# Order of the RWKV-7 projections and of the work between them and the recurrence

## The chip, the cores and the metric
The kernel runs on one core of a Trainium2 chip. The time is device microseconds of one launch. The time before is the median of three runs.

## The reference
One step of a 4-layer recurrent decoder trunk in float32, for a prompt of 256 tokens and 8 samples of 4 tokens that share the weights (288 token columns in the kernel, D = 1024). The layers' token mixers are RWKV-7, gated DeltaNet, HGRN2 and RWKV-7 again; each is followed by a gated convolution FFN. Only the two RWKV-7 mixers (layers 0 and 3, j = 0 and 1 in the code) matter here:

```python
mixed = x[None] + (prev - x)[None] * P['rwkv_mix'][j][:, None, None, :]
xr, xw, xk, xv, xa, xg = (mixed[s] for s in range(6))
r, k, v = jnp.einsum('sbtd,sde->sbte', jnp.stack([xr, xk, xv]), P['rwkv_w_rkv'][j])
w_log = -softplus(-(w0 + tanh(xw @ w1) @ w2)) - 0.5
a = sigmoid(a0 + (xa @ a1) @ a2)
v = v + (v_first - v) * sigmoid(v0 + (xv @ v1) @ v2)        # layer 3 only
g = sigmoid(xg @ g1) @ g2
kk = _l2norm(hd(k * k_k))
k = k * (1 + (a - 1) * k_a)
decay = jnp.exp(-jnp.exp(w_log))
o, S = _rwkv7_scan(hd(r), hd(decay), hd(k), hd(v), kk, hd(a), S0)
bonus = jnp.sum(hd(r) * hd(k) * r_k, -1, keepdims=True) * hd(v)
```

## The kernel before, in words
Activations lie in SBUF as eight row tiles of 128 features by 288 columns; a whole activation is 128 x 2304. A 1024 x 1024 weight is read as four slabs of 128 x 2048 (256 output columns, 1 MB). `weight_plan` fixes the order of all slabs; SyncE loads them in that order into a ring of four slots, each as soon as TensorE is through with the slab four places earlier. A large projection is made with three rounded matmuls: ScalarE copies a slab's high half (`split_hi`, tile `w_hi`, two slots), VectorE subtracts it to get the low half (`split_lo`, tile `w_lo`), and TensorE makes high x high, high x low and low x high for each of the 8 x 2 blocks (`three`, lines 532 to 534). ScalarE evacuates each output tile (`evac`). The input of such a projection, a mixture of the normed input and its shifted neighbour, is split by VectorE in the same way (`split_tiles`). The small projections (w1/w2 for the decay, a1/a2, g1/g2, in layer 3 also v1/v2 for the gate of v) are plain float32 matmuls (`linear_slab`, line 483), the second of each pair waiting for ScalarE's activation of the first.

Every engine's order is the order of its code, in `rwkv(j)` of each engine's block. Before, it is: v, (v1, v2 in layer 3), k, r as twelve slabs, then w1, w2, a1, a2, g1, g2; then the chain that makes the operands of the recurrence. VectorE scales k by `k_k` (`kk_raw`); ScalarE squares it; TensorE sums per head with a block matrix of ones (`tile_stats`, line 554), ScalarE takes logarithm and exponential (`head_rstd`, signal `rk_ready`); VectorE makes the running sums of the decay's logarithm (`tensor_tensor_scan`), the corrected key K, the normed key and B; three exponentials of the running sums come from ScalarE (`e_excl`, `e_incl`, `e_neg`), with VectorE's products and the eight tiles of the bonus between them. `operands_ready` releases TensorE's first products of the recurrence (`invert64`, line 725). The RWKV layers' sample states are loaded by GpSimd's queue, pair by pair, as the recurrence uses them up. GpSimd builds masks at the start of the program and keeps the shift rows; it has no arithmetic in an RWKV layer.

## Time and profile before

| | us |
|---|---|
| median of 3 runs (2378.93 to 2386.48) | 2384.39 |
| profiled execution, own time | 2372.57 |
| its span | 2370.8 |
| TensorE busy (matmul) | 2054.4 (87%) |
| VectorE busy | 1490.4 (63%) |
| ScalarE busy | 959.7 (40%) |
| GpSimd busy | 537.0 (23%) |

The span runs from the first to the last instruction. Busy times are shares of the whole program; a stage is read in windows of the timeline. The granted clock is TensorE's, as a share of its full speed; its mean here is 0.927. Layer 0's RWKV mixer begins the program; layer 3's begins at about 1700 us. An arrow names what ended an idle time.

### The profile page before, as it was taken

The page shows a single profiled execution, that of the slowest core. Times are in us where ns is not written, and L with a number is a line of the kernel's source. Part 1 is how long each engine was busy: PE and PEld are TensorE (multiplying, and loading weights), DVE is VectorE, ACT ScalarE, POOL GpSimd, SP SyncE. Part 2 cuts the span into 40 slices and gives each one's busy share as a digit, 9 for nine tenths or more (in the row PEclk, how much of TensorE's full clock was granted, in tenths as well). Part 3 has the DMA queues.
Part 4 walks back from the last instruction along what each step waited for, and adds up shares of the span by engine and source line. Part 5 has one row for each costly group of instructions (what it writes and reads, how often), then busy time and mean ns, then how long its engine had stood idle before and what let it go on. Part 6 is the DMA issues. An engine that isn't in the chain of part 4 may idle for free.

```text
span 2370.8 us, 54800 instructions
## 1 busy us (share of the span) xinstructions
PE 2054.4 (87%) x23495; PEld 1899.2 (80%) x23495; DVE 1490.4 (63%) x2234; ACT 959.7 (40%) x1640; POOL 537.0 (23%) x931
## 2 busy tenths in 40 slices
PE   4885996899989788799989697999888599869997
PEld 4865885899959677699989676999778388759997
DVE  4547535799368556589645765897465654458972
ACT  3341124555346502455445325555433411344543
POOL 8000000255014121046200550363000000004530
PEclk8987998999989889899999899999989789989999
DMA  4520112354424332244535253454433101224552
GB/s 123 158 63 4 29 37 87 110 171 161 149 81 131 98 99 80 81 160 161 165 115 156 88 168 97 129 171 153 142 112 100 36 21 31 66 72 143 161 165 76
DMA packets 272064, 257.77 MB, mean 109 GB/s; under 512 B 30692, under 2 KB 267206, under 8 KB 271822
## 3 DMA queue, kind: packets, MB, share of 16 engines
q1 hardware_dynamic: 221520, 219.63, 28.9%
q10 hardware_dynamic: 45774, 20.31, 3.2%
q0 software_dynamic: 4528, 14.33, 2.2%
q8 instruction: 186, 3.05, 0.5%
q14 instruction: 56, 0.46, 0.1%
HBM read 235.69 MB, written 18.54 MB: 107 GB/s over the span
## 4 chain that ended last, share of the span: by engine, by line
PE 52%; DVE 7%; ACT 3%; issue 2%; ACTq 0%; POOL 0%; DMA 0%; DVEq 0%; POOLq 0%
PE wide L532 6%; PE bank L532 6%; PE wide L534 6%; PE wide L533 6%; PE bank L534 6%; PE bank L533 6%; DVE arena L2448 3%; PE wide L543 2%; PE wide L752 1%; PE wide L767 1%; DVE arena L2445 1%; ACT arena L1709 1%; PE wide L764 1%; ACT w_hi L1709 1%; PE wide L554 1%
## 5 line engine op out<-in xcount | busy, mean ns | idle before, releaser
L2448 DVE TENSOR_TENSOR w_lo<-ring,w_hi 128x2048 fp32r<-128x2048 f32 (+1 forms) x208 | 471.1, 2268 | 323.1 <-ACT w_hi L1709 320.5
L532 PE MATMUL wide<-arena_rounded,w_hi 128*128 128x288 f32 x1632 | 496.5, 304 | 74.3 <-DVE arena_rounded L2448 57.6
L532 PE MATMUL bank<-arena_rounded,w_hi 128*128 128x288 f32 x1632 | 496.3, 304 | 33.2 <-issue 20.8
L533 PE MATMUL bank<-arena_rounded,w_hi 128*128 128x288 f32 x1632 | 491.3, 301 | 0.0
L534 PE MATMUL bank<-arena_rounded,w_lo 128*128 128x288 f32 x1632 | 490.2, 300 | 0.0
L533 PE MATMUL wide<-arena_rounded,w_hi 128*128 128x288 f32 x1632 | 489.9, 300 | 0.0
L534 PE MATMUL wide<-arena_rounded,w_lo 128*128 128x288 f32 x1632 | 488.3, 299 | 0.0
L1709 ACT ACTIVATE w_hi<-ring 128x2048 fp32r<-128x2048 f32 (+1 forms) x208 | 391.3, 1883 | 138.8 <-PE bank L534 71.4
L532 PEld LDWEIGHTS wide<-arena_rounded,w_hi 128*128 128x128 f32 x1632 | 314.1, 192 | 85.5 <-issue 81.0
L532 PEld LDWEIGHTS bank<-arena_rounded,w_hi 128*128 128x128 f32 x1632 | 316.0, 194 | 36.1 <-issue 35.4
L2445 DVE SCALAR_TENSOR_TENSOR arena<-arena,pv 128x304 f32<-128x304 f32 (+3 forms) x528 | 311.2, 599 | 37.1 <-PE wide L534 21.4
L533 PEld LDWEIGHTS bank<-arena_rounded,w_hi 128*128 128x128 f32 x1632 | 316.0, 194 | 0.5
L534 PEld LDWEIGHTS bank<-arena_rounded,w_lo 128*128 128x128 f32 x1632 | 316.3, 194 | 0.0
L534 PEld LDWEIGHTS wide<-arena_rounded,w_lo 128*128 128x128 f32 x1632 | 315.0, 193 | 0.0
L533 PEld LDWEIGHTS wide<-arena_rounded,w_hi 128*128 128x128 f32 x1632 | 314.5, 193 | 0.4
L1709 ACT ACTIVATE arena<-wide 128x256 f32<-128x256 f32 (+3 forms) x348 | 109.9, 346 | 430.2 <-PE wide L534 258.2
L2448 DVE TENSOR_TENSOR arena<-arena 128x32 f32<-128x32 f32 (+7 forms) x311 | 189.4, 635 | 62.3 <-ACT arena L1709 48.5
L1709 ACT ACTIVATE arena<-bank 128x32 f32<-128x32 f32 (+3 forms) x291 | 83.9, 323 | 322.5 <-PE bank L534 192.6
L1709 ACT ACTIVATE arena<-arena 128x288 f32<-128x288 f32 (+5 forms) x341 | 173.8, 542 | 57.8 <-DVE arena L2448 36.0
L3478 POOL COPY arena<-arena 128x16 f32<-128x16 f32 (+1 forms) x200 | 155.6, 778 | 183.4 <-DVE arena L2445 169.8
L3519 POOL DMA_DIRECT2D sraw<-in_state_rwkv_wkv x32 | 22.1, 694 | 528.1 <-PE wide L1042 281.9
L3487 POOL COPY arena<-arena 128x2 f32<-128x2 f32 (+1 forms) x200 | 92.1, 461 | 178.1 <-ACT arena L1709 172.0
(464 smaller groups left out, 2687.3 us busy)
## 6 DMA issues: line engine op xcount, KB each, us to landing
ring<-in_ffn_w_up SPq DMA_DIRECT2D x88, 1024.0 KB, 5.1
ring<-in_ffn_w_down SPq DMA_DIRECT2D x32, 896.0 KB, 4.8
ring<-in_rwkv_w_rkv SPq DMA_DIRECT2D x24, 1024.0 KB, 5.2
ring<-in_ffn_w_down SPq DMA_DIRECT2D x16, 1024.0 KB, 5.4
ring<-in_gdn_w_in SPq DMA_DIRECT2D x16, 1024.0 KB, 5.7
ring<-in_hgrn_w_in SPq DMA_DIRECT2D x16, 1024.0 KB, 5.5
ring<-in_rwkv_w_o SPq DMA_DIRECT2D x8, 1024.0 KB, 5.8
sraw<-in_state_rwkv_wkv POOLq DMA_DIRECT2D x32, 128.0 KB, 3.0
```

Source lines behind the costliest of these rows:

```text
L532: nc.tensor.matmul(out, wh, xh, start=first, stop=False)
L533: nc.tensor.matmul(out, wh, xl, start=False, stop=False)
L534: return nc.tensor.matmul(out, wl, xh, start=False, stop=last)
L543: mm = nc.tensor.matmul(bk[b][:, 0:T], ones[:, :], src[:, c, :], start=(c == 0), stop=(c == KC - 1))
L554: mm = nc.tensor.matmul(bk[b][:, 0:T], weights[:, :], src[:, c, :], start=True, stop=True)
L752: mm = nc.tensor.matmul(bk[b][rows, c * 64:c * 64 + 64], LT[g][rows, c, :], TF[g][rows, c, :], start=True, stop=True)
L764: nc.tensor.matmul(bk[b][rows, c * 32:c * 32 + 32].rearrange("p (b t) -> p b t", t=h), tt_[g][rows, c, :], halves(EL[g][rows, c, :], h, 0) ...
L1709: return nc.scalar.activation(out, in_, f, bias=bias, scale=scale)
L2445: return V.scalar_tensor_tensor(out=out, in0=a, scalar=s, in1=b, op0=o0, op1=o1)
L2448: return V.tensor_tensor(out, a, b, op)
L3478: G.tensor_copy(s[:, :, 0:lead], hv[:, :, :, c]).then_inc(signal("hist_in"), 1)
L3487: G.tensor_copy(lv[:, 0, :, c], ext[:, NPR:NPR + lead])
```

## The change
The plan and the code of each engine put w1/a1, w2/a2 and g1 first, then k, (v1,) v and r, and g2 last. The weights of v2 are no longer part of a slab: ScalarE's queue loads them into the free tiles `rs` and `nu`. The head statistics of k stand in TensorE's order behind the first v slab. The squares take `k_k` as ScalarE's scale, without VectorE's scaled copy, and ScalarE makes 1 + (a - 1) k_a. VectorE makes the mixtures for k and r in three small tiles (`mixture`) and their splits straight from there; its products, scans and the normed key stand between the low halves of the slabs. The constant 0.6065 goes into the exponentials' scale. The products of K and B with the negative exponential, and in layer 3 the three operations that mix v with the first layer's v, are made by GpSimd on 128 x 2304 tiles. The operands A and R lie in `AR` by operand, tile and column, no longer interleaved by chunk, and R's product with the inclusive exponential is made tile by tile, each followed by its bonus product.

```diff
     def rwkv(j):
-        plan.extend(("rkv", j, 2, m) for m in range(4))
-        if j:
-            plan.append(("v12",))
-        plan.extend(("rkv", j, 1, m) for m in range(4))
-        plan.extend(("rkv", j, 0, m) for m in range(4))
         plan.append(("wa1", j))
         plan.append(("wa2", j))
         plan.append(("g1", j))
+        plan.extend(("rkv", j, 1, m) for m in range(4))
+        if j:
+            plan.append(("v1",))
+        plan.extend(("rkv", j, 2, m) for m in range(4))
+        plan.extend(("rkv", j, 0, m) for m in range(4))
         plan.append(("g2", j))
...
-        lora = tm[:, 0, 0:T]
+        hidden = [tm[:, :, :].rearrange("p a b -> p (a b)")[:, i * T:(i + 1) * T] for i in range(3)]
+        v2 = [t[:, :, :].rearrange("p a b -> p (a b)") for t in (rs, nu)]
...
-        ARp = flat("A6", 2)[:, 0:4096].rearrange("p (c n q t) -> p c n q t", c=KC, n=NCH, q=2)
-        ARs = flat("A6", 2)[:, 4096:4608].rearrange("p (c q t) -> p c q t", c=KC, q=2)
+        AR = flat("A4", 2).rearrange("p (q c t) -> p q c t", q=2, c=KC)
...
@@ block.tensor, rwkv(j) @@
...
+                square_linear(4, "SQ", "A8", ("k", j), "mix_split")
+                if j:
+                    wv1 = slab()[:, 0:256].rearrange("p (k n) -> p k n", k=8)
+                    kv = linear_slab(lambda k, q: wv1[:, k, :], lambda k: S[3][:, k, :], 1, ("v1", j), "mix_split", m=32)
+                    free_after(filled["scalar"], kv + 1)
+                for s in range(4):
+                    i = split_slab_tiles("A5", "A0", "mix_split" if s == 0 and not j else None)
+                    mark[("v", j), 2 * s], mark[("v", j), 2 * s + 1] = i - 1, i
+                    if s == 0:
+                        tile_stats(bones, "square_ready", src=S[7])
...
+                square_linear(4, "SQ", "A8", ("r", j), "mix_split")
...
+                tile_stats(bones, "bonus_product", "vector", src=H)
+
+                pe.wait_ge(sem("operands_ready"), after(pe, "operands_ready", KC))
+                pe.wait_ge(sem("keys_scaled"), after(pe, "keys_scaled", 2))
                 invert64(j, 0, first_fill(j))
@@ block.scalar, rwkv(j) @@
...
+                for s in range(4):
+                    project(S[4], 0, s)
+                for c in range(KC):
+                    fn(S[7][:, c, :], S[4][:, c, :], ACT.Square, scale=pcol("k_k", j, c)).then_inc(signal("square_ready"), 1)
+                if j:
+                    evac(hidden[0][0:32, :], m=32)
+                project(S[3], 4, 0)
+                head_rstd(S[7], 1.0, 0)
+                project(S[3], 4, 1)
+                act.wait_ge(sem("mix_split"), after(act, "mix_split", 3 * KC))
+                for c in range(KC):
+                    ins = fn(S[2][:, c, :], S[1][:, c, :], ACT.Identity, bias=omka[:, j, c:c + 1], scale=pcol("k_a", j, c))
+                ins.then_inc(signal("a_lin"), 1)
...
+                project(S[3], 4, 2)
+                project(S[3], 4, 3)
+                if j:
                     for c in range(KC):
-                        evac(dst[:, c, :])
...
+                        evac(S[0][:, c, :], ACT.Sigmoid, pcol("v0", 0, c))
+                    log_and_exp()
...
+                project(S[5], 8, 0)
+                act.wait_ge(sem("ge_ready"), after(act, "ge_ready"))
+                fn(S[6], S[6], ACT.Exp, scale=-RW_DECAY).then_inc(signal("e_excl"), 1)
+                project(S[5], 8, 1)
+                act.wait_ge(sem("a_done"), after(act, "a_done"))
+                fn(S[6], S[7], ACT.Exp, scale=RW_DECAY).then_inc(signal("e_neg"), 1)
+                fn(S[7], S[7], ACT.Exp, scale=-RW_DECAY).then_inc(signal("e_incl"), 1)
@@ block.vector, rwkv(j) @@
...
+                for c in range(KC):
+                    mix(S[5][:, c, :], 3, c).then_inc(signal("mix_ready"), 1)
+                for c in range(KC):
+                    mix(S[0][:, c, :], 4, c).then_inc(signal("mix_ready"), 1)
+                split_lo(slabs[0])
+                for c in range(KC):
+                    mix(S[3][:, c, :], 5, c).then_inc(signal("mix_ready"), 1)
+                split_mix(1, "SQ", "A8", {KC + 1: 1})
+                dve.wait_ge(filled["scalar"], mark[("g1", j), 0] + 1)
+                split_mix(0, "A5", "A0", {2: 2, 6: 3, KC + 1: 4}, [S[3][:, c, :] for c in range(KC)])
+                dve.wait_ge(filled["scalar"], mark[("k", j), KC - 1] + 1)
+                split_mix(2, "SQ", "A8", {3: 5, KC: 6})
+                K, B, Vv, R = S[2], S[1], S[3], S[5]
+                dve.wait_ge(sem("a_lin"), after(dve, "a_lin"))
+                tt(K, S[4], K).then_inc(signal("keys_made"), 1)
+                split_lo(slabs[7])
...
+                split_lo(slabs[8])
                 dve.wait_ge(sem("vector_chain"), told["vector_chain"])
+                stt(B, B, -1.0, S[4]).then_inc(signal("keys_made"), 1)
...
+                tt(S[6], S[7], S[6], ALU.subtract).then_inc(signal("ge_ready"), 1)
+                split_lo(slabs[10])
+                dve.wait_ge(sem("e_excl"), after(dve, "e_excl"))
+                tt(S[4], S[4], S[6]).then_inc(signal("a_done"), 1)
+                split_lo(slabs[11])
...
+                    tt(R[:, c, :], R[:, c, :], S[7][:, c, :]).then_inc(signal("operands_ready"), 1)
+                    if c == 0:
+                        dve.wait_ge(sem("keys_scaled"), after(dve, "keys_scaled", 2))
...
+                    stt(H[:, c, :], R[:, c, :], pcol("r_k", j, c), K[:, c, :]).then_inc(signal("bonus_product"), 1)
@@ block.gpsimd @@
+            def scaled_keys(j):
+                if j:
+                    pool.wait_ge(sem("v_first_back"), 16)
+                    pool.wait_ge(drained["scalar"], mark[("v2", j, KC - 1), 0] + 1)
+                    G.tensor_tensor(H, H, S[3], ALU.subtract).then_inc(signal("gpsimd_chain"), 1)
...
+                    G.tensor_tensor(H, H, S[0], ALU.mult).then_inc(signal("gpsimd_chain"), 1)
...
+                    G.tensor_tensor(S[3], S[3], H, ALU.add).then_inc(signal("gpsimd_chain"), 1)
...
+                pool.wait_ge(sem("e_neg"), after(pool, "e_neg"))
+                pool.wait_ge(sem("keys_made"), after(pool, "keys_made", 2))
+                G.tensor_tensor(S[2], S[2], S[6], ALU.mult).then_inc(signal("keys_scaled"), 1)
+                G.tensor_tensor(S[1], S[1], S[6], ALU.mult).then_inc(signal("keys_scaled"), 1)
```

VectorE in layer 0, before, from the second half of the slabs to the recurrence. `w_lo<-ring,w_hi` is a low half; 128x288 is one of eight tiles, 128x2304 a whole activation.

```order
L2445 SCALAR_TENSOR_TENSOR arena<-arena,pv 128x288 x8
L2448 TENSOR_TENSOR w_lo<-ring,w_hi 128x2048 x2
L2445 SCALAR_TENSOR_TENSOR arena<-arena,pv 128x288 x16
L2452 TENSOR_SCALAR arena<-arena,pv 128x288 x8
L2452 TENSOR_SCALAR arena<-arena 128x2304
L2611 SCALAR_TENSOR_TENSOR arena<-seg64,arena 128x288 x8
L2453 TENSOR_SCALAR arena<-arena,pv,omka 128x288 x8
L2448 TENSOR_TENSOR arena<-arena 128x2304 x4
L2445 SCALAR_TENSOR_TENSOR arena<-arena,pv 128x288 x8
```

The same place now, from the end of r's mixture to the copies of the decay.

```order
L2442 TENSOR_TENSOR arena_rounded<-tm,arena_rounded 128x288
L2442 TENSOR_TENSOR arena<-arena 128x2304
L2442 TENSOR_TENSOR w_lo<-ring,w_hi 128x2048
L2439 SCALAR_TENSOR_TENSOR arena<-arena,pv 128x288 x8
L2442 TENSOR_TENSOR w_lo<-ring,w_hi 128x2048
L2439 SCALAR_TENSOR_TENSOR arena<-arena 128x2304
L2618 SCALAR_TENSOR_TENSOR arena<-seg64,arena 128x288 x4
L2442 TENSOR_TENSOR w_lo<-ring,w_hi 128x2048
L2621 SCALAR_TENSOR_TENSOR arena<-seg64,arena 128x288 x4
L2442 TENSOR_TENSOR arena<-arena 128x2304
L2442 TENSOR_TENSOR w_lo<-ring,w_hi 128x2048
L2442 TENSOR_TENSOR arena<-arena 128x2304
```

The last five low halves had nothing but mixtures between them and all products behind them; now the product for K, the normed key, B, the scans, the difference of sums and the decay product stand one by one ahead of a low half.

TensorE in layer 0, before, where the head statistics stood (`arena,bones`; the 16 are those of the key norm and of the bonus).

```order
L483 MATMUL bank0<-tm,ring 128x288
L483 MATMUL bank1<-tm,ring 128x288
L483 MATMUL wide0<-tm,ring 128x288
L559 MATMUL wide2<-ident,spo 72x128
L554 MATMUL wide1<-arena,bones 128x288 x16
L725 MATMUL wide0<-arena 64x64 x16
```

TensorE in layer 0 now, at the end of the first v slab and the beginning of the second.

```order
L533 MATMUL bank0<-arena_rounded,w_hi 128x288
L534 MATMUL bank0<-arena_rounded,w_hi 128x288
L535 MATMUL bank0<-arena_rounded,w_lo 128x288
L555 MATMUL wide1<-arena,bones 128x288 x8
L533 MATMUL bank1<-arena_rounded,w_hi 128x288
L534 MATMUL bank1<-arena_rounded,w_hi 128x288
L535 MATMUL bank1<-arena_rounded,w_lo 128x288
```

The eight key statistics moved from behind all projections to between two slabs; the eight for the bonus stayed behind g2.

GpSimd in layer 0, before, from its last mask to the FFN's history.

```order
L3433 MEMSET mark_cell 128x1
L3509 COPY spo<-arena 128x8
L3510 COPY spo<-arena 128x8x8
L3519 DMA sraw<-in_state_rwkv_wkv 64x8x64 x16
L3446 DMA sraw<-in_state_ffn_conv 88x8x128
```

GpSimd now, at the same place.

```order
L3504 COPY spo<-arena 128x8
L3505 COPY spo<-arena 128x8x8
L3516 DMA sraw<-in_state_rwkv_wkv 64x8x64 x4
L3535 TENSOR_TENSOR arena<-arena 128x2304
L3536 TENSOR_TENSOR arena<-arena 128x2304
L3516 DMA sraw<-in_state_rwkv_wkv 64x8x64 x12
L3441 DMA sraw<-in_state_ffn_conv 88x8x128
```

Two whole products stand between the state loads of the first two head pairs and those of the other six.

## Rows read from the trace of the kernel before

**Rows 1.** Windows of layer 0 and 3: from:to, us, busy us (x instructions), granted clock, DMA.
```profile
45.00:134.00 89.00, 82.73 (x578) 82.05 (x579) 51.14 (x86) 28.78 (x34) 10.74 (x24) 0.93 0.44 132
134.00:166.00 32.00, 27.89 (x97) 17.41 (x95) 21.10 (x42) 16.71 (x32) 0.00 (x0) 0.89 0.26 83
166.00:208.00 42.00, 15.01 (x40) 8.02 (x42) 25.29 (x28) 15.34 (x21) 0.00 (x0) 0.66 0.00 1
...
1722.00:1829.00 107.00, 94.32 (x612) 88.75 (x613) 61.47 (x97) 34.73 (x44) 2.83 (x5) 0.90 0.36 112
```

**Rows 2.** Timeline of TensorE, layer 0: start us, us, engine, line, operation, tiles.
```profile
133.69 4.09 PE L483 MATMUL bank<-arena,ring 128*64 128x288 f32 x16
...
146.44 5.35 PE L483 MATMUL bank<-arena,ring 128*64 128x288 f32 x16
...
207.57 1.97 PE L725 MATMUL wide<-arena 64*64 64x64 f32 x32 [8.56 <-DVE arena L2445]
```

**Rows 3.** Timeline of ScalarE, layer 0.
```profile
28.57 2.77 ACT L1709 ACTIVATE arena<-arena 128x288 f32<-128x288 f32 x8
...
115.11 1.92 ACT L1709 ACTIVATE w_hi<-ring 128x2048 fp32r<-128x2048 f32 x1
...
127.46 0.41 ACT L1709 ACTIVATE arena<-bank 128x288 f32<-128x288 f32 x1 [2.85 <-PE bank L534]
...
133.86 0.41 ACT L1709 ACTIVATE arena<-wide 128x288 f32<-128x288 f32 x1 [2.79 <-PE wide L534]
...
140.46 1.28 ACT L1709 ACT_TABLE_LOAD   x1 [0.90 <-PE bank L483]
...
143.36 1.03 ACT L1709 ACTIVATE arena<-bank,pv 128x288 f32<-128x288 f32 x2
...
169.93 1.01 ACT L1709 ACTIVATE arena<-wide,eps 128x288 f32<-128x288 f32 x2
...
176.77 0.50 ACT L1709 ACTIVATE arena<-wide,eps 128x288 f32<-128x288 f32 x1 [0.24 <-PE wide L554]
...
177.30 2.12 ACT L1709 ACTIVATE arena<-arena 128x2304 f32<-128x2304 f32 x1
```

**Rows 4.** Timeline of VectorE, layer 0.
```profile
42.49 0.95 DVE L2445 SCALAR_TENSOR_TENSOR arena<-arena,pv 128x288 f32<-128x288 f32 x2
...
51.02 2.28 DVE L2448 TENSOR_TENSOR w_lo<-ring,w_hi 128x2048 fp32r<-128x2048 f32 x1
...
148.54 5.31 DVE L2611 TENSOR_TENSOR_SCAN arena<-seg,arena 128x288 f32<-128x288 f32 x8
...
163.55 2.56 DVE L2448 TENSOR_TENSOR arena<-arena 128x2304 f32<-128x2304 f32 x1
...
187.19 3.51 DVE L2445 SCALAR_TENSOR_TENSOR arena<-arena,pv 128x288 f32<-128x288 f32 x8
...
193.28 0.95 DVE L2448 TENSOR_TENSOR arena<-wide,arena 128x288 f32<-128x288 f32 x2
...
199.61 2.63 DVE L2448 TENSOR_TENSOR arena<-arena 128x2048 f32<-128x2048 f32 x2
```

**Rows 5.** Timeline in the HGRN2 layer: first VectorE, then GpSimd.
```profile
1302.61 4.39 DVE L2448 TENSOR_TENSOR arena<-arena 128x2304 f32<-128x2304 f32 x1
...
1302.48 2.11 POOL L3568 TENSOR_TENSOR arena<-arena 128x1152 f32<-128x1152 f32 x1
...
1304.67 4.30 POOL L3566 TENSOR_TENSOR arena<-arena 128x1152 f32<-128x1152 f32 x1
```

**Rows 6.** Timeline in layer 3: first VectorE, then TensorE.
```profile
1715.75 3.52 DVE L2445 SCALAR_TENSOR_TENSOR arena<-arena,pv,rstd 128x288 f32<-128x288 f32 x8 [1.96 <-ACT rstd L1709]
...
1897.05 3.43 PE L725 MATMUL wide<-arena 64*64 64x64 f32 x64 [8.57 <-DVE arena L2445]
```

**Rows 7.** Start: a timeline row of TensorE, then a window.
```profile
18.99 0.61 PE L559 MATMUL wide<-ident,arena 128*128 128x128 f32 x2 [18.99 <-DMA arena<-in_state_rwkv_shift]
...
2.10:19.10 17.00, 0.11 (x1) 0.14 (x2) 0.00 (x0) 0.00 (x0) 13.93 (x46) 1.00 1.07 323
```

More of the change, by code:

```diff
@@ L1888, in rwkv @@
             def rwkv(j):
-                n0 = plan.index(("rkv", j, 2, 0))
-                slabs = [plan.index(("rkv", j, q, m)) for q in (2, 1, 0) for m in range(4)]
-                pre_norm(n0)
-                def project(dst, first):
-                    for c in range(KC):
-                        evac(dst[:, c, :])
-                        if c % 2 and first + c // 2 + 2 < len(slabs):
-                            split_hi(slabs[first + c // 2 + 2])
-                project(S[3], 0)
+                slabs = [plan.index(("rkv", j, q, m)) for q in (1, 2, 0) for m in range(4)]
@@ new lines, in rwkv, with project @@
+                if j:
+                    squares(X, "x_ready")
+                rms()
+                split_hi(slabs[0])
+                def project(dst, first, s):
+                    for c in (2 * s, 2 * s + 1):
+                        evac(dst[:, c, :])
+                    if first + s + 2 < len(slabs):
+                        split_hi(slabs[first + s + 2])
+                hear_conv_out()
+                if j:
+                    for q in range(2):
+                        act.dma_start(v2[q][0:32, :], A["rwkv_v2"][0][:, q * 512:(q + 1) * 512]).then_inc(sem("v2_landed"), 16)
@@ new lines, in split_mix @@
+                def split_mix(i, hi, lo, at, full=mixture):
+                    n = len(full)
+                    for step in range(KC + 2):
+                        if 1 <= step <= KC:
+                            dve.wait_ge(sem("tile_made"), after(dve, "tile_made"))
+                            V.tensor_copy(act3r(hi)[:, step - 1, :], full[(step - 1) % n]).then_inc(signal("tile_hi"), 1)
+                        if step < KC:
+                            if step >= n:
+                                dve.wait_ge(sem("mix_split"), told["mix_split"])
+                            elif step == 0 and "mix_split" in told:
+                                dve.wait_ge(sem("mix_split"), told["mix_split"])
+                            mix(full[step % n], i, step).then_inc(signal("tile_made"), 1)
+                        if step >= 2:
+                            dve.wait_ge(sem("tile_hi"), after(dve, "tile_hi"))
+                            tt(act3r(lo)[:, step - 2, :], full[(step - 2) % n], act3r(hi)[:, step - 2, :],
+                               ALU.subtract).then_inc(signal("mix_split"), 1)
+                        if step in at:
+                            split_lo(slabs[at[step]])
@@ new lines, in rwkv @@
+                split_lo(slabs[9])
+                for c in range(4, KC):
+                    ins = V.tensor_tensor_scan(S[7][:, c, :], seg64[:, :], S[6][:, c, :], 0.0, ALU.mult, ALU.add)
+                ins.then_inc(signal("vector_chain"), 1)
+                dve.wait_ge(sem("vector_chain"), told["vector_chain"])
+                tt(S[6], S[7], S[6], ALU.subtract).then_inc(signal("ge_ready"), 1)
+                split_lo(slabs[10])
+                dve.wait_ge(sem("e_excl"), after(dve, "e_excl"))
@@ L2628, in rwkv @@
-                for c in range(KC):
-                    stt(SQ[:, c, :], R[:, c, :], pcol("r_k", j, c), K[:, c, :]).then_inc(signal("bonus_product"), 1)
-                dve.wait_ge(sem("e_excl"), after(dve, "e_excl"))
-                tt(ARp[:, :, :, 0, :], blocks64(KK), blocks64(S[2]))
-                tt(ARs[:, :, 0, :], KK[:, :, NPR:T], S[2][:, :, NPR:T]).then_inc(signal("a_done"), 1)
-                dve.wait_ge(sem("a_done"), told["a_done"])
+                    dve.wait_ge(drained["scalar"], mark[("r", j), c] + 1)
```

234 lines of the change are left out of this document (77 added, 157 removed).

## The prediction, made before the changed kernel ran

> **What bounds the kernel now.** I read the windows of the two RWKV layers first, then the timeline of each engine there. The table by windows shows three stretches per layer. Under the twelve weight slabs TensorE is busy 82.7 of 89 us in layer 0 and 94.3 of 107 us in layer 3. Under the small projections it is busy 27.9 of 32 us. In the 42 us before the recurrence it works 15 us, VectorE 25, ScalarE 15, DMA nothing, and TensorE's mean granted clock is 0.66 [rows 1]. No engine is full there: key norm, decays and products hand over from one engine to the next. In the TensorE timeline this stretch ends at 207.57, where the first 64-wide products start, having waited 8.56 us on VectorE [rows 2]; in layer 3 at 1897.05 [rows 6]. So the target is a serial chain of about 42 us twice, while VectorE has about 38 idle us under the slabs of layer 0 (89 less 51.1) and 45 under those of layer 3 [rows 1]. The work on both ends of a stage is a chain too: what shortens the stage moves everything behind it.
>
> **Prices.** One slab takes 6.40 us at the high clock (127.46 to 133.86 for its two tiles). Its high half costs ScalarE 1.92, an evacuated tile 0.41, a table load 1.28, two sigmoid tiles 1.03 (with gaps 0.533 each), eight plain activations 2.77, one exponential over all eight tiles 2.12, and the eight logarithms with their statistics 7.34 (169.93 to 177.27) [rows 3]. VectorE: low half 2.28, a mixture with its split over eight tiles 8.5 (42.49 to 51.02), scans 5.31, a whole product 2.56, eight scalar products 3.51, eight bonus evacuations 6.3 (193.28 to 199.61) [rows 4]. Eight fp32 matmuls with 288 columns take 4.09 at the high clock and 5.35 where it was partly low, so a spell at the low level costs about 1.3 [rows 2].
>
> **Layer 0 step by step**, all on the clock of the trace of before, starts held.
> (1) The first mixture starts at 42.5 as now. TensorE comes from a pause, so w1 costs between 4.1 and twice that; I give it 6.6 us, and a1 4.1: 53.7. (2) ScalarE evacuates, loads the sigmoid table and does sixteen sigmoids: 53.9 + 0.4 + 1.3 + 16 x 0.533 = 64.1. TensorE follows it, g1 can start at 62.6 and ends at 66.7; with the small transpose the first k slab starts at 67.3. Its mixture (16 mixtures, low half, 8 mixtures, 8.5 of split) is ready at 64, so it is covered. (3) Slabs k0 to k3 and v0: 5 x 6.4 = 32.0, to 99.3. Slab k1 can be loaded only when a1 is through, at 54; it has 20 us. (4) TensorE's queue now holds the eight key statistics between v0 and v1. ScalarE must evacuate two tiles and split slab v2 first (2 x 0.41 + 1.92), then comes 6.7 of the 7.34, all but the last logarithm: TensorE is free at 108.8, a stop of 9.5 us. (5) v1: 6.4 and 0.7, half a spell of low clock, 115.9. (6) VectorE waits for the linear form of a (ScalarE: evacuation 0.4, high half 1.9, eight activations 2.8), multiplies K (2.6), and only then makes the low half of v3 (2.3). That half is ready at 115.9 + 10.0 = 125.9, v2 ends at 122.3: a stop of 3.6, then v3 ends at 132.3, and 133.6 with 1.3 for a low clock. (7) VectorE's work between the low halves of v3 and r3 is 3.5 + 2.3 + 2.55 + 5.3 + 2.3 + 2.56 + 2.3 + 2.56 + 2.3 = 25.7 us, against 25.6 for four slabs; so the low halves come just in time, and r3 ends at 159.4. g2 takes 4.2, to 163.6. (8) In that queue the scans end at 141.8, the difference of sums at 144.4, the low half of r2 at 146.6, the product with the exclusive decay at 149.1; ScalarE's negative exponential follows at 151.4, and GpSimd then multiplies K and B.
>
> GpSimd's price is not in the trace for 2304 elements. The nearest row is 2.11 us for 1152 [rows 5], so 4.2 us for one; from below 2.56, what VectorE takes [rows 4], from above 8.6, twice the 4.30 of one that was blocked. I take 4.2: the keys are scaled at 160.3. (9) Then VectorE makes eight pairs of R and bonus product, each 0.44 + 0.475 (3.51 / 8 and 0.95 / 2) [rows 4], all but the first product of R behind the scaled keys: 7.0 to 167.4; then 6.3 of bonus evacuation, whose last statistic frees TensorE at 173.1. The recurrence starts at 173.1 instead of 207.57: 34.5 us gained. Both ends: if the clock stays high and nothing is late, steps (1), (5), (6) and (9) give 6 back, 40; if GpSimd takes 8.6 each, 8.8 are lost, 26.
>
> The same seen from the slabs: the last r tile is evacuated at 133.86 now [rows 3], 73.7 us ahead of the recurrence. With the small projections in front r3 ends 25.5 later, but only 13.7 lie behind it: 60.0 - 25.5 = 34.5.
>
> **What row and rule say of GpSimd beside VectorE.** A VectorE product of 2304 elements that started at 1302.61 took 4.39 us instead of 2.56; beside it GpSimd's product ran from 1302.48 to 1304.59. Then GpSimd's next product, 1304.67, took 4.30 instead of 2.11, and VectorE's product had ended at 1307.00 [rows 5]. So two-input instructions of both wait for each other whole. The Trainium skill (SBUF — State Buffer, Who interferes with whom) states this: the shared port pair is an exclusive lock, and a VectorE instruction with two SBUF inputs blocks against a GpSimd instruction that reads SBUF. The trace agrees. It speaks against this change, because VectorE's low halves of slabs are such instructions.
>
> **Layer 3.** Same steps, with more. The mixture starts 6.5 behind the norm's first row at 1715.75 [rows 6], at 1722.25 now. The high half of the first slab no longer stands ahead of the squares (1.92 [rows 3]); 1.8 of it I count, so 1720.4, an offset of 1677.9 against layer 0. k3 ends at 1770.8; the rank-32 product is 4.1 more, v0 ends at 1781.3, TensorE is free of the statistics at 1790.3, v3 ends at 1815.1. New here is v's gate: table load, eight sigmoids, then eight small matmuls that follow ScalarE, so r0 starts at 1821.8. The three GpSimd products for v run from 1823.4, 4.2 each, and alternate with VectorE: difference of sums done at 1830.2, low half of r2 at 1836.7 (r1 ended at 1834.6: stop 2.1), product with the decay 1843.5, low half of r3 1845.8 (r2 ended 1843.1: stop 2.7), r3 ends 1853.5 with 1.3 for the clock. Negative exponential 1845.6, keys scaled at 1854.4, pairs 1861.6, recurrence at 1867.3 instead of 1897.05: 29.8 gained. Ends: without blocking 36; with GpSimd at 8.6 and all five products in line 22 less, 8.
>
> ScalarE's table loads go from two to five in layer 3 (stay three in layer 0) by the order of instructions; three more at 1.28 are in the times above. By the Trainium skill (ScalarE: Activation LUTs, What ACT_TABLE_LOAD costs) a load also drains for about 1.38 us, some 2.66 together. From the load at 140.46 to the fourth sigmoid at 143.36 are 2.90 us, of which three sigmoids are 1.6, so 1.3 are left for the load and no drain is seen [rows 3]; by the rule the sum would be some 4 us less.
>
> **Start.** SyncE's first four slabs were 4 MB, now 0.5 + 0.5 + 0.5 + 1 MB. From 2 to 19 us the DMA engines are full at 323 GB/s, and TensorE's first transposes wait until 18.99 for the last parameter [rows 7]. 1.5 MB less is at most 4.9 us; the parameter is issued at 12 us itself, and small rows move slower, so between 0 and 4.9; I take 3. SyncE's order behind it holds nothing new: its ring has room. GpSimd's masks end at 51, ahead of the first use of its shift rows.
>
> **Costed at nothing:** the new layout of the A and R operands (columns in two pieces; TensorE streams the same count; bounds plus or minus 2 us), the state loads of pairs behind GpSimd's products (they wait for the recurrence anyway, which begins later), the removed scaling of the decay (1.4 us, out of the chain already removed), reading v first into H instead of A8 (four slabs of cover), the weights of v's gate on ScalarE's queue (ahead of its tanh, which waits for w1 anyway). None lies on the path of the sum.
>
> **Sum:** 34.5 + 29.8 + 3 = 67.3. The profiled execution took 2372.6 (span 2370.8 and 1.8 around it); it would become 2305.3. The median of before is 2384.4, 11.8 above it; I forecast 2384.4 - 67.3 = 2317.1, rounded 2317. Its own range, from ends of the unknown costs that don't all fall one way, is 2303 to 2335.
>
> **Rivals.**
> A, the slabs pay: the moved work lies ahead of low halves in VectorE's queue (25.7 us against 25.6, so no reserve). If handovers or GpSimd make each of v3, r0, r1, r2, r3 late by 4 us, and each stop costs 1.3 of low clock, that is 5 x 5.3 = 26.5 per layer, where I have 5 and 11 already: 37 less, 2354. For it: the blocked rows [rows 5]. Against it: 4 us late at every slab would need 16 us more of work or waits than my rows give for those four slabs.
> B, more than the sum: the stop in (4) overlaps better, the clock stays at its high level through the small projections, and GpSimd's products miss VectorE's. That is the sum of the upper ends, 40 + 36 + 4.9 = 81: 2303; with other chains shortened below that, 2298.
> C, slower than before: the clock. The stops (9.5, 3.6 and the gaps of the small projections) keep TensorE at 1.2 GHz. A slab then takes up to 12.8 us instead of 6.4. It decides from 11 of the 24 slabs on (11 x 6.4 = 70, more than the sum); with 16 it is 102 - 67 = 35 slower, 2419. Against it: 0.93 and 0.90 are the clocks of the slab stretches now, with 6.3 and 12.7 us of stops among them [rows 1].
> D, it does less than it says: the chain is not hidden but goes on behind r3, on a slower engine, with GpSimd's products at 8.6 each. Gain 26 + 8 + 3 = 37, 2347. For it: GpSimd never did so wide a product with VectorE beside it; against it: 2.11 for half the size, alone.
>
> **Chances.** Forecast 0.62, A 0.10, B 0.14, C 0.03, D 0.11. The range that holds 8 in 10 takes the forecast's own, B's near end and D: 2300 to 2347. What a measurement can tell from no change is 0.3%, 7 us. Faster 0.96 (all but C and 0.01 of A), same 0.01, slower 0.03.
>
> **What would show it.** Right: TensorE's first w1 matmul at about 40 (start gained), the first k slab 24 to 26 us behind it, a stop of 9 to 10 us for eight statistics behind v0, a stop of 3 to 4 us before v3, the two GpSimd products at 4.2 us each between the negative exponential and the bonus pairs, 13 to 14 us from r3's end to the recurrence, and that start 34 us earlier in layer 0 (without the gain at the start) and, counted between the norm and the recurrence, about 28 in layer 3. Everything behind each layer unchanged to 2 us. Wrong: GpSimd rows above 6 us, low halves that end 4 us after the slab before in r0 and r1, slabs longer than 8 us, or a later stage that gives time back.

## The result and the profile after

| | before | changed |
|---|---|---|
| median, first comparison (4 runs each) | 2384.0 | 2326.4 (2318.11 to 2333.28) |
| ratio, 95% interval | | 0.976 (0.972 to 0.980) |
| median, second comparison (9 and 4 runs) | 2382.98 | 2330.22; 0.978 (0.976 to 0.980) |
| span of the profiled execution | 2370.8 | 2316.3 |
| mean granted clock | 0.927 | 0.937 |

The change gains 53 to 58 us; 67 were forecast. The profiled executions differ by 54.5 us of span, and they are compared here stage by stage. First the stages by windows of the changed kernel: from:to, us, busy us of PE, PEld, DVE, ACT and POOL (x instructions), granted clock, DMA share, GB/s. In layer 0 they are the small projections, k0 to v0, the key statistics, v1 to r3, and what is left ahead of the recurrence.

```profile
42.00:66.00 24.00, 22.23 (x82) 13.10 (x83) 21.53 (x53) 10.09 (x19) 12.14 (x25) 0.91 0.38 107
66.00:98.00 32.00, 32.00 (x242) 32.00 (x241) 23.74 (x41) 18.50 (x25) 0.00 (x0) 1.00 0.52 169
98.00:106.00 8.00, 5.57 (x25) 3.37 (x24) 6.54 (x14) 6.45 (x12) 0.00 (x0) 1.00 0.42 131
106.00:158.00 52.00, 46.90 (x333) 46.58 (x333) 36.75 (x27) 27.21 (x31) 8.71 (x2) 0.93 0.42 135
158.00:173.30 15.30, 10.06 (x31) 5.98 (x29) 11.47 (x24) 3.32 (x9) 1.63 (x1) 0.78 0.00 0
...
1689.00:1718.00 29.00, 27.65 (x80) 16.86 (x81) 21.08 (x50) 10.10 (x19) 2.79 (x5) 0.72 0.28 91
```

What lay before 166 in [rows 1], slabs and small projections, now ends at 158, statistics included, and the 42 us behind it, with TensorE working 15 of them, are now 15.3. The last row is the same stretch as the first, but in layer 3: 29 us at a clock of 0.72, where layer 0 needs 24 at 0.91. A granted clock of 1.00 is 2.4 GHz, 0.50 is 1.2 GHz, the low level; a low spell below is a stretch at that level, and a share in between is a mean over both.

TensorE's timeline in layer 0 answers to [rows 2]. The brackets give the idle time ahead of the instruction and what ended it.

```profile
43.29 9.38 PE L484 MATMUL bank<-arena,ring 128*64 128x288 f32 x32 [8.24 <-DVE arena L2439]
...
100.99 1.26 PE L555 MATMUL wide<-arena,bones 128*128 128x288 f32 x4 [2.01 <-ACT arena L1700]
...
123.07 0.58 PE L533 MATMUL bank<-arena_rounded,w_hi 128*128 128x288 f32 x1 [5.11 <-issue]
...
167.68 5.71 PE L555 MATMUL wide<-arena,bones 128*128 128x288 f32 x12 [5.24 <-DVE arena L2442]
173.31 0.86 PE L714 MATMUL wide<-arena 64*64 64x64 f32 x22
```

The recurrence begins at 173.31 (207.57 before), and three stops are left: among the statistics, 5.11 before slab v3, and 5.24 before the bonus statistics. The middle one reads "issue": no semaphore event is shown for it. VectorE's timeline, which answers to [rows 4], shows its cause.

```profile
118.21 2.56 DVE L2442 TENSOR_TENSOR arena<-arena 128x2304 f32<-128x2304 f32 x1 [13.67 <-ACT arena L1700]
120.69 2.29 DVE L2442 TENSOR_TENSOR w_lo<-ring,w_hi 128x2048 fp32r<-128x2048 f32 x1
...
147.22 2.29 DVE L2442 TENSOR_TENSOR w_lo<-ring,w_hi 128x2048 fp32r<-128x2048 f32 x1 [0.52 <-ACT w_hi L1700]
151.25 3.36 DVE L2630 COPY cen<-arena 128x32 f32<-128x32 f32 x1 [1.73 <-ACT arena L1700]
154.53 5.18 DVE L2631 COPY els<-arena 128x64 f32<-128x64 f32 x1
159.63 0.44 DVE L2442 TENSOR_TENSOR arena<-arena 128x288 f32<-128x288 f32 x1
```

VectorE idles 13.67 us for the linear form of a, makes the product for K, and only then the low half that TensorE waits for. The linear form itself is eight activations of ScalarE (its timeline):

```profile
113.94 4.24 ACT L1700 ACTIVATE arena<-arena,omka,pv 128x288 f32<-128x288 f32 x8
```

At the end of VectorE's rows two copies of 32 and 64 elements a row take 3.36 and 5.18 us. GpSimd's timeline of the same stretch, then of layer 3:

```profile
149.29 5.27 POOL L3535 TENSOR_TENSOR arena<-arena 128x2304 f32<-128x2304 f32 x1 [93.61 <-ACT arena L1700]
154.50 5.13 POOL L3536 TENSOR_TENSOR arena<-arena 128x2304 f32<-128x2304 f32 x1
...
1796.17 6.83 POOL L3527 TENSOR_TENSOR arena<-arena 128x2304 f32<-128x2304 f32 x1 [104.07 <-ACT arena L1700]
1803.07 5.18 POOL L3529 TENSOR_TENSOR arena<-arena 128x2304 f32<-128x2304 f32 x1
1808.33 7.12 POOL L3531 TENSOR_TENSOR arena<-arena 128x2304 f32<-128x2304 f32 x1
```

The copies end where GpSimd's products end. In layer 3 VectorE's product with the decay, 2.56 alone, took 7.54 beside the third of them:

```profile
1810.33 7.54 DVE L2442 TENSOR_TENSOR arena<-arena 128x2304 f32<-128x2304 f32 x1
```

**Where the 54.5 us lie.** This table gives the lead over the kernel before at places that both traces have. The splits are ScalarE's high halves of weight slabs.

| place | before | changed | lead |
|---|---|---|---|
| first transpose | 18.99 | 19.04 | 0 |
| recurrence, layer 0 | 207.57 | 173.31 | 34.3 |
| next split behind it | 367.76 | 338.64 | 29.1 |
| last split of layer 2's FFN | 1689.80 | 1658.66 | 31.1 |
| norm's first row, layer 3 | 1715.75 | 1682.71 | 33.0 |
| recurrence, layer 3 | 1897.05 | 1843.57 | 53.5 |
| last split of all | 2338.44 | 2283.97 | 54.5 |

Layer 0's recurrence gives 5.1 back. In it TensorE's clock was low for most of 8 us, which the kernel before did not have there. Here are windows of TensorE in the changed kernel (us, PE busy, granted clock, DMA share, GB/s):

```profile
209.00:217.00 8.00, 8.00 (x135) 0.57 0.02 4
173.00:209.00 36.00, 31.88 (x1226) 1.00 0.07 19
```

### The profile page after: what moved, and what is told of

It reads as the page before. It is cut to its first block, busy times and chain, and to the rows that moved or that the text cites. A ratio compares the mean times of both kernels' runs of the same rounds, so it can differ in the third digit from the quotient of the medians.

```text
span 2316.3 us, 54804 instructions
## 1 busy us (share of the span) xinstructions
PE 2045.1 (88%) x23495; PEld 1890.1 (82%) x23495; DVE 1485.1 (64%) x2217; ACT 972.4 (42%) x1659; POOL 575.7 (25%) x938
## 4 chain that ended last, share of the span: by engine, by line
PE 51%; DVE 7%; ACT 3%; issue 2%; POOL 0%; ACTq 0%; DMA 0%; DVEq 0%; POOLq 0%
PE wide L533 6%; PE bank L533 6%; PE wide L534 6%; PE wide L535 6%; PE bank L534 6%; PE bank L535 6%; DVE arena L2442 3%; PE wide L544 2%; ACT arena L1700 1%; DVE arena L2439 1%; PE wide L756 1%; PE wide L741 1%; PE wide L753 1%; ACT w_hi L1700 1%; PE wide L484 1%
## 5 line engine op out<-in xcount | busy, mean ns | idle before, releaser
L2439 DVE SCALAR_TENSOR_TENSOR arena<-arena,pv 128x304 f32<-128x304 f32 (+2 forms) x512 | 303.2, 601 | 15.5
L2442 DVE TENSOR_TENSOR arena<-arena 128x288 f32<-128x288 f32 (+7 forms) x312 | 173.0, 580 | 63.1 <-ACT arena L1700 49.2
L1700 ACT ACTIVATE arena<-arena 128x288 f32<-128x288 f32 (+6 forms) x325 | 168.7, 548 | 40.4 <-DVE arena L2442 20.7
L2439 DVE SCALAR_TENSOR_TENSOR arena<-arena,pv,rstd 128x288 f32<-128x288 f32 x128 | 61.8, 511 | 109.8 <-ACT rstd L1700 109.7
```

The costliest lines, as they stand in the source:

```text
L1700: return nc.scalar.activation(out, in_, f, bias=bias, scale=scale)
L2439: return V.scalar_tensor_tensor(out=out, in0=a, scalar=s, in1=b, op0=o0, op1=o1)
L2442: return V.tensor_tensor(out, a, b, op)
```

## The experiments

The times of one kernel move by 5 to 15 us with such spells, so each experiment is read by a length of its stage: from the start of slab k2's high half to the recurrence. The changed kernel has 100.3 us there in layer 0 and 118.3 in layer 3, and 100.3 and 119.7 in its repeat; so a difference under 1.5 us in layer 3 tells nothing. Where an interval is given, the kernel was timed in four or five executions beside the kernel before.

| | layer 0 | layer 3 | median of runs | ratio to before |
|---|---|---|---|---|
| changed (repeat, e5) | 100.3 | 119.7 | 2330.22 | 0.978 (0.976 to 0.980) |
| e1, products on VectorE | 94.6 | 112.1 | 2321.34, one run | |
| e6, the same | 94.7 | 112.1 | 2315.14 | 0.971 (0.969 to 0.973) |
| e4, matmuls in the pause | 100.1 | 118.5 | 2318.13, one run | |
| e2, low half first | 97.1 | 116.5 | 2318.51, one run | |
| e3, chain behind | 117.6 | 131.7 | 2355.77, one run | |
| e9, statistics halved | 98.8 | 118.0 | 2327.72, one run | |
| e7, all on VectorE | 82.1 | 96.2 | 2288.08 | 0.960 (0.959 to 0.961) |
| e8, parameters first | 82.1 | 96.2 | 2286.54 | 0.959 (0.958 to 0.961) |
| e10, e8 with gate first | 82.1 | 96.8 | 2273.65 | 0.955 (0.953 to 0.957) |
| e11, gate first alone | 101.8 | 119.6 | 2321.34 | 0.975 (0.974 to 0.977) |

**e3: the order without the hiding.**
```diff
+                split_lo(slabs[7])
...
+                split_lo(slabs[11])
                 dve.wait_ge(sem("a_lin"), after(dve, "a_lin"))
                 tt(K, S[4], K).then_inc(signal("keys_made"), 1)
-                split_lo(slabs[7])
...
                 tt(S[4], S[4], S[6]).then_inc(signal("a_done"), 1)
-                split_lo(slabs[11])
```
ScalarE's three exponentials move behind its last slab in the same way.

> Order of projections as in the changed kernel, but VectorE's and ScalarE's chain (K product, normed key, B, scans, difference, product with the decay, the exponentials) stands behind the low half of r3 instead of between the low halves. Theory 1: hiding the chain under the slabs is worth most of the gain that the new order does not give by itself: TensorE's stops before v3 and before r2 and r3 of layer 3 go (r3 ends about 5 us earlier in layer 0, 8 in layer 3), but 23 us of chain and 10.4 of GpSimd follow, so each recurrence starts 16 to 18 us later than in the changed kernel: 2350 of span. Rival: what counts is only that the small projections stand in front, and the time stays within 5 us of the changed kernel.

The stage is 17.3 and 13.4 us longer, the whole 37.7 (6.6 of it a low spell ahead of layer 0's slabs). TensorE now waits 22.8 us in one piece ahead of the bonus statistics (waits of e3 in layer 0: engine, line, releaser, us in total, times, longest):

```profile
PE wide L555 <- DVE arena L2437: 22.8, 1, 22.8
...
PE wide L555 <- DVE arena L2440: 4.6, 1, 4.6
```
The rival falls. By these two stages hiding the chain is worth about 31 us of the 54. What is left, some 24 us, is put down to the new order and the shorter chain together; no run has either alone.

**e1 and e6: the two products back on VectorE.**
```diff
+                tt(K, K, S[6]).then_inc(signal("keys_scaled"), 1)
+                tt(B, B, S[6]).then_inc(signal("keys_scaled"), 1)
...
                 V.tensor_copy(dec64, S[7][:, :, CH - 1:NPR:CH])
...
-                G.tensor_tensor(S[2], S[2], S[6], ALU.mult).then_inc(signal("keys_scaled"), 1)
-                G.tensor_tensor(S[1], S[1], S[6], ALU.mult).then_inc(signal("keys_scaled"), 1)
```


> The products of K and B with the negative exponential go back to VectorE (ahead of the two small copies), in both layers; GpSimd keeps only the three products for v in layer 3. Theory 1: GpSimd's 2304-element products took 5.1 to 5.3 us and held up every VectorE instruction beside them, the 32- and 64-element copies too (3.4 and 5.2 us). Then VectorE makes both in 5.1 us from 149.5, the copies take 0.2 each, the first R product starts at 155.0 instead of 159.63, and layer 0's recurrence at about 168.7 instead of 173.31; in layer 3 the R product starts 4.7 us earlier. 9 us less in all: about 2307 beside 2316 of span. Theory 2: GpSimd did work that VectorE had no room for, and the copies are slow for a reason of their own (strided source): then the copies stay above 3 us and nothing or a loss comes of it.

> The two products for K and B on VectorE, timed. Counted from the high half of the last r slab, the first look had each recurrence 6.6 and 6.2 us earlier than the changed kernel, but a low granted clock elsewhere hid it. Theory 1 (GpSimd's products and the lock are the price of this part): 13 us less than the changed kernel beside it, about 0.994 of it. Rival (the time that is saved is given back where the recurrence begins earlier): within 3 us of it.

VectorE's timeline of e6 in layer 0:

```profile
155.34 2.29 DVE L2442 TENSOR_TENSOR w_lo<-ring,w_hi 128x2048 fp32r<-128x2048 f32 x1 [0.52 <-ACT w_hi L1700]
157.55 5.02 DVE L2442 TENSOR_TENSOR arena<-arena 128x2304 f32<-128x2304 f32 x2
162.49 0.18 DVE L2634 COPY cen<-arena 128x32 f32<-128x32 f32 x1
162.58 0.21 DVE L2635 COPY els<-arena 128x64 f32<-128x64 f32 x1
162.71 0.45 DVE L2442 TENSOR_TENSOR arena<-arena 128x288 f32<-128x288 f32 x1
```
Both products and both copies take 5.2 us (157.55 to 162.71); with GpSimd the same stretch took 10.3 (149.29 to 159.63). The strided-copy explanation falls: the same copies take 0.18 and 0.21. The stage is 5.7 and 6.2 us shorter. e1's single run was 3 us above the changed kernel's profile, for its small projections in layer 0 and a stretch of the gated DeltaNet had low spells. e6's median is 15.1 us below that of the changed kernel timed beside it (13 expected), and the intervals don't touch.

**e2: the low half first.**
```diff
+                split_lo(slabs[7])
                 dve.wait_ge(sem("a_lin"), after(dve, "a_lin"))
                 tt(K, S[4], K).then_inc(signal("keys_made"), 1)
-                split_lo(slabs[7])
```


> The low half of slab v3 is made ahead of the product for K instead of behind it. Theory 1: VectorE's queue is full from there to r3, so TensorE's stop of 5.1 us before v3 goes (v3 starts at about 118.1 instead of 123.07), but a new stop of about 2 us or more opens before r0 or r1, because VectorE's own chain begins only about 2.1 us earlier; per layer 2 us are gained, 4 in all. Theory 2: the slabs bound the stage, and the full 5.1 us per layer comes back, 10 in all.

The stop before v3 is gone in layer 0. A new one stands before r0 (TensorE's timeline of e2):

```profile
126.60 0.37 PE L533 MATMUL wide<-arena_rounded,w_hi 128*128 128x288 f32 x1 [2.33 <-issue]
```
The stage is 3.2 and 1.8 us shorter, not 5.1. In layer 3 one stop of 8.2 us replaces 5.1 and 3.0. Theory 1 holds: 5.0 us over both layers, where it had 4 and its rival 10.

**e9: the statistics halved.**
```diff
-                    if s == 0:
-                        tile_stats(bones, "square_ready", src=S[7])
+                    if s < 2:
+                        tile_stats(bones, "square_ready", src=S[7], tiles=range(4 * s, 4 * s + 4), banks=4)
```


> The changed kernel with its key statistics in two halves of four, behind v0 and behind v1, over four banks of PSUM; nothing else is moved. Theory 1 (stops in a row are not a sum: what ends last before v3 is the linear form of a on ScalarE, the product for K and only then the low half): TensorE's wait of 2.7 us among the statistics goes, but ScalarE now has four logarithms and the exponential, 4.2 us, ahead of the linear form, so the low half of v3 is ready at about 122.3 instead of 122.98 and v3 starts less than 1 us earlier; 1 to 2 us less over both layers. Rival (each stop that is taken away is time gained): v3 and all that follows start 2.7 us earlier in each layer, 5 us less.

v1 came 5.2 us earlier, since half of the statistics moved behind it, but before v3 TensorE then waited longer, 7.45 (its timeline in e9):

```profile
130.90 0.58 PE L533 MATMUL bank<-arena_rounded,w_hi 128*128 128x288 f32 x1 [7.45 <-issue]
```
1.5 us were left in layer 0 and 0.2 in layer 3, where such a difference can't be told from none. The rival's 2.7 falls: two stops in a row with one cause behind the second are not a sum.

**e5, e7 and e8: everything at once, and the start.**
```diff
+                for c in range(KC):      # scans into the free H, while the statistics run
+                    ins = V.tensor_tensor_scan(H[:, c, :], seg64[:, :], S[6][:, c, :], 0.0, ALU.mult, ALU.add)
...
+                    tt(S[7], S[7], Vv, ALU.subtract).then_inc(signal("vector_chain"), 1)   # v's gate, layer 3
...
+            sync.wait_ge(sem("params_landed"), 16 * PARAM_DMAS)                            # e8 only
             for n, key in enumerate(plan):
```


> The changed kernel itself, for the spread that the clock makes. In the profiles so far the same instructions of the small projections of layer 0 ran 6.5 us longer in two of five executions, those of the gated DeltaNet stretch 134 to 144 us. If these spells fall by chance, the times scatter by 5 to 15 us round 2326; if the profiled 2318 was the normal one and the others were disturbed, the median comes near 2318.

> New order of VectorE's and ScalarE's work with nothing on GpSimd: key statistics in two halves behind v0 and v1, over four banks instead of two; scans into the free H while the statistics run; the linear form of a ahead of slab v1's evacuation; low half of v3 as soon as its high half is there; products of v, K and B on VectorE; bonus product in the buffer of the key norm. Theory 1 (what the changed kernel still loses is stops that the order makes: 7.6 + 5.1 us in layer 0, 7.4 + 5.1 + 3 in layer 3, and GpSimd's 10.4 in each): no stop over 3 us between k0 and r3, recurrence of layer 0 at 155 to 160 instead of 173.3, counted from the first k slab 91 instead of 107, that of layer 3 counted from its first k slab about 102 instead of 125. 35 to 40 us less in all, about 2280 to 2290. Rival (VectorE is full under the slabs, so what leaves GpSimd makes the low halves late): stops of 3 to 5 us before r1 to r3, and less than 15 us gained.

> As e7_all_on_vector, and SyncE loads the first weight slabs only when all parameters have landed, so that the parameters have the DMA engines to themselves after x. Theory 1 (the start is DMA-bound): TensorE's first transpose at 14 to 16 us instead of 19.04, 3 to 5 us less in all, and w1 still finds its weights (needed at 39). Rival (the start waits for the issue of 28 parameter loads and for small packets, whatever else is moved; it was 19.0 with 5.96 MB and 19.0 with 4.39 MB): no change within 1 us.

The changed kernel scatters from 2325 to 2337 in e5, and the time goes with the mean granted clock: 0.931 at 2325.22, 0.928 at 2336.70, and 0.937 at the 2318.11 of the first comparison. The profiled 2318 was a favourable execution. In e7 TensorE has no stop over 0.3 us from the first k slab of layer 0 to the recurrence at 155.45 (the stage of layer 3 has one of 2.2 us). Windows of e7 from the first k slab on:

```profile
66.00:143.00 77.00, 76.67 (x561) 75.29 (x560) 64.94 (x81) 51.45 (x64) 0.00 (x0) 1.00 0.51 164
143.00:155.50 12.50, 12.50 (x70) 10.54 (x68) 10.64 (x26) 4.11 (x10) 0.00 (x0) 1.00 0.23 78
```
The stages are 18.2 and 22.0 us shorter than in the changed kernel's profile, the time 42 us less than in e5. The rival falls: VectorE had the room for the three products for v and the two for the keys.

In e8 the first transpose starts 6.1 us earlier than in e7, so the weights' loads held the parameters up; w1 starts at 36.73 instead of 43.58. But the first k slab gains only 0.7: the small projections had a low spell that e7's had not. The times differ by 1.5 us, less than their intervals tell apart, so of theory 1 the start is shown and the 3 to 5 us in all are not. TensorE's timeline of e8, the start and two groups of the spell:

```profile
13.13 0.61 PE L560 MATMUL wide<-ident,arena 128*128 128x128 f32 x2 [13.13 <-DMA arena<-in_state_rwkv_shift]
...
52.40 1.85 PE L484 MATMUL wide<-tm,ring 64*128 64x288 f32 x4
54.05 2.12 PE L484 MATMUL bank<-tm,ring 64*128 64x288 f32 x4
```

**e4, e10 and e11: the low clock of the small projections.** In the changed kernel layer 3's w1 starts at 1689.88 and its first k slab at 1718.16, 28.3 us; in layer 0 the same work takes 22.5 (43.29 to 65.83).
```diff
+                for _ in range(30):                                              # e4
+                    nc.tensor.matmul(bk[b][:, 0:P], ident[:, :], ident[:, :], start=True, stop=True)
...
-        plan.append(("wa2", j))                                                  # e10, e11
         plan.append(("g1", j))
+        plan.append(("wa2", j))
```


> Thirty extra 128x128 matmuls of the identity, with no reader, fill TensorE's pause before w1 in both layers (8.3 us idle in layer 3). Theory 1: the low granted clock in the small projections (0.54 in 1708 to 1716) follows from the pause before them, so it stays at 1.00, g1 takes 4.1 instead of 5.25 us, and the first k slab of layer 3 starts about 6 us earlier counted from the norm's first row (29.8 instead of 35.6), layer 0 about 2 us. Rival: the second low spell, which came after sixteen matmuls at the high level, has nothing to do with the pause; then only the 2.4 us of w1 come back in each layer and 1704 to 1716 stays low.

> As e8_params_first, with the product for the gate (g1, 128 rows) ahead of w2 and a2 (64 rows each) in all queues. In every run so far layer 3's w2 and a2 ran at about half the granted clock, in layer 0 they did in four of nine profiles, and always the same way for the same kernel. Theory 1 (those sixteen small matmuls with their handovers to ScalarE bring the low level about): with g1 in front, the matmuls of w2 and a2 run low again, wherever they now stand, and the first k slab begins as late as before, within 1.5 us. Rival (the low spell comes some time behind the pause ahead of w1, whatever runs then): g1 itself, 4.1 us at the high level, takes up to 8 us, w2 and a2 take their 9.3 us.

> The changed kernel with g1 ahead of w2 and a2 in all queues and nothing else. In e10_gate_first the matmuls of w2 and a2 ran at the high level in both layers. Theory 1 (the 0.47 us pause between the first tiles of w2 and a2 and what led up to it made the low spell of layer 3; g1 fills it): layer 3's first k slab comes 30 to 32 us behind the norm's first row instead of 35.6, layer 0 stays within 1 us, and the time is 4 to 5 us below the changed kernel. Rival (e10 was high because its layers begin at another moment): layer 3's w2 and a2 are low again and nothing changes within 2 us.

TensorE in layer 3 of e4, as windows (us, PE busy, granted clock, DMA share, GB/s):

```profile
1692.00:1708.00 16.00, 13.94 (x73) 1.00 0.24 77
1708.00:1720.00 12.00, 12.00 (x26) 0.50 0.09 32
```
The extra matmuls keep the pause at work and w1 at the high level (4.07 instead of 6.51 us), but w2 and a2 fall to the low one all the same, and sooner. Theory 1 of e4 falls; of its rival's 2.4 us, 0.9 are left at layer 3's first k slab. In e10 and e11 both theories of e10 fall: within the small projections nothing behind w1 is low any more, in either layer. Here are rows of w2 and a2 in layer 3, of the changed kernel and then of e11. An fp32 matmul leaves two records here, so each row of four is two matmuls:

```profile
1708.11 2.12 PE L484 MATMUL bank<-tm,ring 64*128 64x288 f32 x4
1710.03 2.12 PE L484 MATMUL wide<-tm,ring 64*128 64x288 f32 x4
```
```profile
1713.70 1.23 PE L484 MATMUL bank<-tm,ring 64*128 64x288 f32 x4
1714.80 1.21 PE L484 MATMUL wide<-tm,ring 64*128 64x288 f32 x4
```
In e11 the first k slab follows w1 by 23.4 us and the norm's first row by 30.6 (35.5 in the changed kernel), as theory 1 expected. But layer 0 did not stay within 1 us: there the first k slab follows w1 by 24.0 us instead of 22.5, the stretch of the key statistics had a low spell (8.2 us instead of 7.0), and the recurrence starts at 175.49, 2.2 later. So e11's span is 2318.2, the changed kernel's 2316.3. The medians of e11 and the repeat are 8.9 us apart across the two comparisons, which ran on different chips, and the intervals of the ratios overlap: the 4.9 us are shown by the trace for this stretch alone, and a gain of the whole by neither. What exactly in the order brings the low level about stays open: with g1 in front the pause of 0.47 us shrinks to 0.19, and the engine has had more 128-row work before. In layer 0 the low spell was there in e1, e3, e6, e8 and e9 and not in the changed kernel, its repeat, e2, e4 or e7. The two kernels that were profiled twice (e1 and e6 are one kernel) gave the same both times; that hints at a cause in the kernel, but two pairs don't show it.

e10 is the fastest version that was run: 0.955 of the kernel before, 2.4% below the changed kernel's repeat.

## Why the forecast was right, and where it was 10 to 15 us too good

The mechanism was right: the chain went under the slabs, and in layer 0 15.9 us lie between r3's end and the recurrence, forecast 13 to 14. The steps:

- **Start, 3 us: 0, at the lower end of what it allowed.** With 4.39 MB instead of 5.96 in the first 26 us the transpose started at 19.04 instead of 18.99. From 4 to 12 us the kernel before moved 337 GB/s; the changed one moved 297, then 225, with rows of 256 and 512 bytes among the loads (2556 packets under 512 bytes, 476 before). The prediction had noted small rows and allowed 0 to 4.9, and then took 3; in e8, with no slab loaded ahead of the last parameter, the transpose started at 13.13.
- **Layer 0, 34.5: right, 34.3, with errors that cancel.** k0 was forecast at 67.3 and came at 65.83. From the end of v0 to the start of v1 the statistics took 7.0 us (97.84 to 104.80) and not 9.5, for the logarithms went in pairs, 1.47 a pair. The stop before v3 was 5.1 and not 3.6: the eight activations of the linear form took 4.24, not 2.8. Slab v3 behind it took 8.7 us at a granted clock of 0.69 (122 to 132), where 7.7 were forecast. r3 ended at 157.4 (159.4). GpSimd's products took 5.27 and 5.13, not 4.2, and the copies that were costed at nothing waited for both; but they started at 149.29 and not at 151.4, so the R products began at 159.63. Steps (8) and (9) came out at 173.3 against 173.1, and so near a hit is luck: 2.1 us early and 2.0 too long. A slip of 0.5 stands in the sum itself (151.4 and two products of 4.2 give 159.8, not 160.3).
- **Layer 3, 28 counted from the norm: wrong, 20.4.** This is the step that failed, by 7.6 us. 4.2 of them lie ahead of k0, which came 35.45 us behind the norm's first row and 31.3 by the prediction's steps: it took layer 0's steps over at "an offset of 1677.9 against layer 0", which supposes layer 0's clock, and here w2, a2 and g1 ran largely at the low level. Against layer 0 as measured that costs 5.8 us; e11 takes 4.9 away. The other 3.3 lie between k0 and the recurrence (125.4 us, forecast 122.1). There slab r0 took 8.9 us at a granted clock of 0.70 (1794 to 1805), where 6.4 were forecast. GpSimd's five products took 5.1 to 7.1 and not 4.2, and a product of VectorE was held up for 5 us; of the stops before r2 and r3 (2.1 and 2.7) only the second came, 3.0. The products for K and B started 1.6 us later against k0 than forecast and took 10.2 instead of 8.4. e6 shows 6 us in this layer for K and B alone.
- **1.8 us for the high half that no longer precedes the squares: right**, 33.0 less 31.1.
- **"Everything behind each layer unchanged to 2 us": wrong in layer 0's recurrence**, where 5.1 us were lost. The low spell is part of it (8 us at 0.57, an estimate of 3.4 us); what made the rest is not shown. From the recurrence's start to the next split all twelve profiles with the new order take longer than the kernel before, 161.9 to 167.0 us against 160.2. It may be the change that makes such spells likelier; the one profile of before doesn't settle it.
- **The lock:** the row agreed with the rule cited, and the copies were still costed as free. In the runs two VectorE copies with one input, 32 and 64 fp32 elements a row, ended only when a GpSimd product had ended. The same section of the Trainium skill (SBUF — State Buffer, Who interferes with whom) says that copies may run in a mode that takes both ports and then block too. The trace agrees that they wait (3.36 and 5.18 us); it doesn't show the mode. The prediction used only the sentence on two inputs.
- **Rule on table loads** (the Trainium skill, ScalarE: Activation LUTs, What ACT_TABLE_LOAD costs): the drain of about 1.38 us beside a load was again not seen, and the measurement decides. In layer 3 the load ran 1790.49 to 1791.77 and the first sigmoid started at 1791.79.
- **Rivals:** A, stops at each slab, did not come: low halves were late before v3 and, in layer 3, r3, and nowhere else. C did not come as a whole, but low spells took part of the 5.1 us in layer 0's recurrence and 4.9 us in layer 3's small projections. D was half right: GpSimd's products took less than 8.6 and more than 4.2, and e6, with two of them back on VectorE, has stages 5.7 and 6.2 us shorter.
- **Signs:** two that the prediction named for being wrong did come, GpSimd rows above 6 us (6.83 and 7.12 in layer 3) and a later stage that gives time back. They cost less than its margin.

## What to carry to other kernels

By these runs, give work to an idle GpSimd only where VectorE is idle too: a product of 2304 fp32 elements a row cost 5.1 us there and stopped VectorE for as long, against 2.56 on VectorE. When a chain is hidden under a stage, look for the last thing ahead of each handover (here a low half queued behind a product that waits for ScalarE), and put what TensorE waits for in front; removing an earlier stop alone gives little. Don't carry a stage's length from one layer to the next without its granted clock.

## What was not expected of the hardware

- VectorE's COPY of 32 or 64 elements a row took 3.4 and 5.2 us beside a GpSimd product and 0.2 without. In e3 the second copy slipped in between two GpSimd products and took 0.20.
- GpSimd's products: 5.04 to 5.27 us for 2304 fp32 elements where VectorE made little beside it, 2.2 ns an element, against 1.83 in the nearest row of before (2.11 for 1152) [rows 5].
- Most of the sixteen fp32 matmuls of w2 and a2 ran at the low level in layer 3 of every changed kernel with g1 behind them, pause filled or not (2.12 us for two), and all at the high level in both kernels with g1 in front (1.23). The cause is open.
- An ACTIVATE over 288 elements took 0.35 with no operand per partition (2.77 for eight), 0.44 with one for the scale (3.50) and 0.53 with scale and bias (4.24).
